# A decoder trunk with eight experts: transposes of the hidden activations in other PSUM banks, one gather at the end of an expert, and a down projection that ends with two pairs of blocks

## What is computed

```
x = x + sliding_window_attention(rms_norm(x, attn_norm), w_qkv, sinks, w_o)
x = x + swiglu(rms_norm(x, ffn_norm), w_gate, w_up, w_down)       # 2816 wide
x = x + pooling_mixer(rms_norm(x, pool_norm), pool_w, scale)      # trailing means, 4 groups
x = x + moe_swiglu(rms_norm(x, moe_norm), router, w_gate, w_up, w_down)
return rms_norm(x, final_norm)

def moe_swiglu(...):        # 8 experts, 3584 wide, the best 2 of each token
    logits = t @ w_router;  top 2;  gates = softmax(top 2)
    out = sum over e of combine[:, e] * ((silu(t @ w_gate[e]) * (t @ w_up[e])) @ w_down[e])
```

## Time and profile before

| | us |
|---|---|
| median of 3 runs | 1147.63 |
| the three runs | 1147.43, 1147.63, 1148.69 |
| the profiled execution | 1149.0 |
| its span in the trace | 1147.2 |
| PE matmul rows busy | 1127.3 (98%) |
| DVE, ACT busy | 313.4 (27%), 138.7 (12%) |
| DMA queue q1 | 83.3% of 16 engines' span |

### The profile page before, as it was taken

The page is one execution under the profiler, slowest core; times in us unless marked ns, Lnnn a source line. Parts: engine busy times, 40 slices in busy tenths (PEclk is TensorE's granted clock), DMA queues, the critical chain, the costliest instruction groups (busy, mean ns, idle before and its releaser), DMA issues.

```text
span 1147.2 us, 14885 instructions
## 1 busy us (share of the span) xinstructions
PE 1127.3 (98%) x6247; PEld 503.4 (44%) x6248; DVE 313.4 (27%) x561; ACT 138.7 (12%) x293; POOL 17.6 (2%) x59
## 2 busy tenths in 40 slices
PE   9999999999999999999999999999999999999997
PEld 8645566764653343353333335333333533333332
DVE  3556865666541110110201011021101101110102
ACT  1452011100131110000101000010100001110001
POOL 2300000000000000000000000000000000000000
PEclk9999999999999999999999999999999999999999
DMA  7535433447298999999999999999999999999995
GB/s 295 221 119 211 152 142 125 181 170 311 116 433 362 385 386 382 431 429 431 429 429 415 418 429 430 428 429 431 431 429 430 428 428 429 429 429 430 429 424 207
DMA packets 19414, 402.92 MB, mean 351 GB/s; under 512 B 3328, under 2 KB 3328, under 8 KB 4224
## 3 DMA queue, kind: packets, MB, share of 16 engines
q1 hardware_dynamic: 19328, 401.67, 83.3%
HBM read 400.61 MB, written 1.05 MB: 350 GB/s over the span
## 4 chain that ended last, share of the span: by engine, by line
PE 90%; DMA 7%; DVE 1%; ACT 1%; issue 0%; SPq 0%; DVEq 0%; ACTq 0%
PE bank L1686 32%; PE bank L1784 13%; PE bank L1447 12%; PE bank L1667 9%; PE bank L1482 6%; PE bank L1805 4%; DMA ring<-moe_w_up 4%; DMA ring<-moe_w_down 3%; PE bank L1394 2%; PE bank L1338 2%; PE bank L1646 1%; PE bank L1628 1%; DMA ring<-attn_w_qkv 1%; PE bank L1305 1%; PE bank L1748 1%; PE bank L1315 1%
## 5 line engine op out<-in xcount | busy, mean ns | idle before, releaser
L1686 PE MATMUL bank<-ring,arena 128*64 128x448 f32 x2048 | 391.3, 540 | 2.0 <-DMA ring<-moe_w_up 2.0
L1686 PEld LDWEIGHTS bank<-ring,arena 128*64 128x64 f32 x2048 | 144.7, 137 | 247.4 <-issue 244.3
L1784 PE MATMUL bank<-ring,arena 128*64 128x512 f32 x896 | 197.3, 595 | 2.5 <-DVE arena L1216 1.5
L1447 PE MATMUL bank<-ring 128*128 128x384 f32 (+1 forms) x448 | 134.4, 459 | 0.0
L1784 PEld LDWEIGHTS bank<-ring,arena 128*64 128x64 f32 x896 | 63.8, 137 | 124.3 <-issue 119.3
L1177 DVE TENSOR_TENSOR arena<-bank,arena 128x448 f32<-128x448 f32 x32 | 20.0, 625 | 332.9 <-PE bank L1686 332.9
L1447 PEld LDWEIGHTS bank<-ring 128*128 128x128 f32 x448 | 84.3, 190 | 45.8 <-issue 0.5
L1667 PE MATMUL bank<-ring,arena 128*32 128x448 f32 x1024 | 99.7, 541 | 0.0
L1227 DVE COPY arena<-bank 64x512 f32<-64x512 f32 x8 | 5.6, 694 | 228.4 <-PE bank L1784 228.4
L1667 PEld LDWEIGHTS bank<-ring,arena 128*32 128x32 f32 x1024 | 31.5, 110 | 66.6 <-issue 66.6
L867 DVE TENSOR_TENSOR ring<-ring 128x1536 f32<-128x1536 f32 (+2 forms) x35 | 53.2, 1540 | 10.3 <-PE bank L1381 9.3
(11 more groups left out here) (211 smaller groups left out, 675.3 us busy)
## 6 DMA issues: line engine op xcount, KB each, us to landing
ring<-moe_w_gate SPq DMA_DIRECT2D x32, 3584.0 KB, 24.3
ring<-moe_w_up SPq DMA_DIRECT2D x32, 3584.0 KB, 27.3
ring<-moe_w_down SPq DMA_DIRECT2D x29, 3584.0 KB, 27.5
ring<-ffn_w_gate SPq DMA_DIRECT2D x3, 3072.0 KB, 11.0
ring<-ffn_w_up SPq DMA_DIRECT2D x3, 3072.0 KB, 10.1
ring<-ffn_w_down SPq DMA_DIRECT2D x3, 3072.0 KB, 10.1
ring<-moe_w_down SPq DMA_DIRECT2D x3, 2048.0 KB, 31.4
ring<-moe_w_down SPq DMA_DIRECT2D x3, 1536.0 KB, 34.5
```

The source lines that it names most:

```text
L1447: last = mm(ffn_bank(m, i), b[lhs][:, k, :], b[rhs][:, k, :], start=k == 0, stop=k == 3)
L1686: last = mm(bank[2 * (j % 2) + up][64 * h:64 * h + 64, 0:FJ], xg[:, k, side:side + BASE], w[:, k, h, :], start=k == 0, stop=k == KD - 1)
L1784: last = mm(bank[2][64 * h:64 * h + 64, :], hg[:, i0 + i, half * BASE:half * BASE + BASE], w[:, i, h * BANK:h * BANK + BANK], start=d == 0 ...
```

## The change

- `STREAMED` is 9 in place of 8: pair 8 runs with the streamed ones, and the last round has two pairs per product, 9 and 10. Pair 9's sums lie in `ring[5]` in place of `nrm`; on DVE `scale_maps` moves behind `combine(9)`.
- The third down chunk is then free at `pair_done`, 9 in place of `prod_done`, 7, and SP loads the first expert's c = 3, which goes into that buffer, ahead of c = 1.
- `turn_banks`: at even places the batches of `hid` go to banks 0, 1, 6, 7 and those of `hidx` to banks 4 and 5; at odd places the banks stay as they were. So at even places batches b >= 2 don't wait for `hidx_ready`; the transposes of `hidx` do. In expert 0 they wait for the first gather's banks to have been read.
- Experts 1, 3, 5: the wait for `xg_ready` stands inside the branch that they don't take (they have no extra tokens). Batch b = 1 waits for the third part of `hid` in place of the fourth.
- Expert 0: the gather for expert 1 and the transposes of the combination weights stand behind the down products, with their copies on DVE (`keep_xg(1, 1)`) and ACT (`keep_combination`) moved likewise.

```
-STREAMED = 8
+STREAMED = 9
...
-HTR_BANK = (0, 1, 4, 5)
+def turn_banks(it):
+    return ((0, 1, 6, 7), (4, 5)) if isinstance(it, int) and it % 2 == 0 else ((0, 1, 4, 5), (6, 7))
...
-        read_by += [(pair_done, 3), (pair_done, 6), (prod_done, 7), (prod_done, 7), (mix_done, 2)]
+        read_by += [(pair_done, 3), (pair_done, 6), (pair_done, 9), (prod_done, 7), (mix_done, 2)]
...
-                for c in (2, 1, *range(3, PER_IT)) if first else range(PER_IT):
+                for c in (2, 3, 1, *range(4, PER_IT)) if first else range(PER_IT):
...
                 if looped:
                     gather(it + 1, 0)
-                elif it == 0:
-                    gather(1, 1)
...
-                    pe.wait_ge(hid_ready, 4 * it + min(b + 3, 4) if b < 2 else 4 * it + 4)
-                    if b >= 2:
+                    pe.wait_ge(hid_ready, 4 * it + (3 if b < 2 else 4))
+                    if b >= 2 and turned[b] < 6:
                         pe.wait_ge(hidx_ready, 4 * it + 4)
+                    elif b >= 2 and not looped and it == 0:
+                        pe.wait_ge(xg_ready, 2)
...
-                elif it < NE - 1:
-                    pe.wait_ge(xg_ready, 4 * ((it + 1) // 2) + 4)
                 with pe.If(ext > 0):
+                    if not looped:
+                        pe.wait_ge(hidx_ready, 4 * it + 4)
+                    if pair:
+                        pe.wait_ge(xg_ready, 4 * ((it + 1) // 2) + 4)
...
                     if d == 1:
                         pe.wait_ge(hgA_ready, 2 * it + 2)
                         pe.wait_ge(hgV_ready, 2 * it + 2)
-                        pe.wait_ge(dispw_ready, 2 * it + 2)
-                        for a in range(2):
...
+                        if looped or it > 0:
+                            combination(it)
...
+                if not looped and it == 0:
+                    combination(it)
+                    gather(1, 1)
                 return ext
```

More of the change, by code:

```diff
@@ L1715, in flag, with combination @@
                 return pe.value_load(one, min_val=0, max_val=1)
+            def combination(it):
+                pe.wait_ge(dispw_ready, 2 * it + 2)
+                if turn_banks(it)[1][0] == 4:
+                    pe.wait_ge(hgxA_ready, it + 1)
+                for a in range(2):
+                    for t in range(T):
+                        last = nc.tensor.transpose(bank[4][:, (2 * a + t) * P:(2 * a + t + 1) * P],
+                                                   dispw[:, t, a * P:a * P + P], ident[:, :])
+                last.then_inc(ctr_done, 1)
             def expert(it, extp, ext, looped=False):
```

33 lines of the change are left out of this document (18 added, 15 removed).

## The result

| | before, us | after, us |
|---|---|---|
| median of 14 runs each, on one chip | 1148.88 | 1150.37 |
| lowest to highest | 1147.43 to 1150.16 | 1148.32 to 1153.06 |
| the profiled execution | 1149.0 | 1150.26 |
| its span | 1147.2 | 1148.5 |

The ratio is 1.0015, with an interval of 1.0008 to 1.0022: by that ratio the changed kernel is 1.7 us slower (0.9 to 2.5), while the two medians differ by 1.5. The forecast was +0.9 us; the sign was right and the size about half of what was measured. The time itself lies just inside the stated range (1145.8 to 1150.4), but this says little: the forecast started from three runs with a median of 1147.63, and over 14 runs the kernel before has 1148.88.

A forecast was written before the change was run, and what follows sets the result against it. The prediction took the weight-chunk stream, last held up by PE at 647 us, as the bound; 1.5 + 0.5 - 0.33 - 0.77 = +0.9 us there gave 1148.5 us, range 1145.8 to 1150.4.

The forecast's parts named there:

- The bound: Whole kernel: a gapless stream of weight chunks to 1129 us sets the end, not PE.
- the anchor: End of expert 2, SP's issue of expert 3's c = 4 at 647.02 us: the stream's last standstill, forecast +0.9 us.
- Rival two: Stream does not hang on 647 us, gaps are transfer jitter, PE's changes vanish in the queue: 1147.6 us; chance 0.12.
- rival three: PE is the bound and the early chunk keeps its lead: -4.05 us, 1143.6 us; chance 0.07.
- The mixer: Mixer's first matmuls behind the last down-projection round: PE stops 1.44 us for the second norm, +1.5 us with the hand-over.
- Rival one: The mixer does not stall, the second norm is in time: anchor at -0.6, 1147.0 us; chance 0.14.
- The early chunk: First expert's c = 3, issued at 294.3 us, 12 us sooner: worth 0, as the queue runs dry at 358 us anyway.
- Expert 0: Gather and combination behind expert 0's down products: expert 1 starts 0.5 us later, bounds 0.3 to 1.0.
- Rival four: Expert 1 waits for its tokens behind DVE's copies: 2.8 us on top in full, 1151.3 us; chance 0.11.
- Odd experts: First down products of experts 1, 3, 5 wait less: -0.33 us each, only expert 1's ahead of the anchor.
- Even experts: Experts 2, 4, 6: batches 3 and 4 fill the `hidx_ready` wait, -0.77 us each, only expert 2's ahead of the anchor.
- The sum: Terms at the anchor, 1.5 + 0.5 - 0.33 - 0.77 = +0.9 us, carried by the stream to the end: 1148.5 us.

The follow-up runs named there:

- ffn_alone: Kernel before with only the down projection's part of the change (two pairs in the last round, early third expert chunk); 1150.96 us, ratio 1.0016.
- no_ffn: Changed kernel with the down projection's part undone (last round and third expert chunk as before), expert part kept; 1148.17 us, ratio 0.9995.
- no_ffn_warm: no_ffn with twelve identity transposes into an unused bank ahead of the last down step; 1148.78 us, ratio 0.9995.
- no_ffn_apart24: no_ffn with the extra down products of experts 2 and 4 also taken step by step, as expert 0's already were; 1146.07 us, ratio 0.9973.
- before_apart2: Kernel before with expert 2's extra down products taken step by step, as expert 0's already were; 1148.40 us, ratio 0.9991.
- gather_early: Changed kernel with expert 0's gather for expert 1 and combination transposes, and their copies, back in their old places; 1151.07 us, ratio 1.0010.
- after_again: The changed kernel itself, unaltered, run again on the chip of warm12_again; 1150.02 us, ratio 1.0010.
- late_chunk: Changed kernel with the first expert's c = 3 loaded as before, behind prod_done, 7 and behind c = 1; 1149.74 us, ratio 1.0008.
- cold: Kernel before with two of eight k-steps of expert 7's last up product left out, so PE waits longer for the last chunk; 1149.91 us, ratio 1.0007.
- no_ffn_apart2: no_ffn with expert 2's extra down products also taken step by step, as expert 0's already were; 1146.87 us, ratio 0.9979.
- warm12_again: Same code as warm12 (twelve filling transposes in the changed kernel), on the same chip as after_again; 1150.06 us, ratio 1.0010.
- no_ffn_apart2_ge: no_ffn_apart2 with expert 0's gather and combination transposes back in their old places; 1148.08 us, ratio 0.9989.
- warm12: Changed kernel with twelve identity transposes into an unused bank ahead of the last down step's wait; 1149.38 us, ratio 1.0005.
- no_ffn_apart: no_ffn with the extra down products of experts 2, 4 and 6 taken step by step, as expert 0's already were; 1147.28 us, ratio 0.9986.

## Why the prediction was right in part

- **The bound.** Right. The stream hangs on PE's time at 647 us: ffn_alone moves the anchor by 1.62 us and the last step by 1.46, no_ffn moves them by -1.16 and -1.64 (no_ffn_warm, though, has only the anchor's part), and with the gaps at the ends of experts 2 and 4 closed (no_ffn_apart24) PE no longer waits for a chunk. Rival two, a stream that does not hang on 647, falls. before_apart2 alone would not show it: its lead is lost again at expert 4, and its ratio, 0.9991, has an interval that reaches 1.0000. But with 2.1 us more work for PE it is not slower, and rival three, PE as the bound, falls by that. The Trainium skill ("Perfetto Trace Analysis", Identifying the Most-Contended Engine) puts the engine with the highest occupancy first, and calls matmul busy time a poor measure on TensorE. By its matmul rows PE is at 98%, yet the traces show that it did not set the time and became the bound only with the splits.
- **The mixer.** The idle time was 1.44 us, as worked out. Rival one falls. At the anchor the edit costs 1.62 to 1.69 us, forecast 1.5.
- **The early chunk.** 0, as said; issued at 294.00, forecast 294.3. The 1.2 us from an issue to its data, used on both sides of that sum, is about 1.0 in the traces.
- **Expert 0.** +0.32 us (gather_early), forecast 0.5. Rival four, a wait for expert 1's tokens, did not come: 445.72 + 3.71 us of gather, and the first product at 449.36.
- **Odd experts.** From the gather's first matmul to the down product, 501.75 to 508.94, it is 7.19 us and was 7.86 (499.90 to 507.76): -0.67, forecast -0.33, outside the bound of -0.5. The forecast had left 0.18 us of idle time ahead of the down product, as in expert 7; none is left in expert 1, and 0.58 us of the gain lies there. The other 0.09 stood ahead of the gather's second half. No run separates the moved wait from the looser wait of batch b = 1.
- **Even experts.** From the first transposes to the down product, expert 2 took 3.98 us (607.97 to 611.95) and takes 3.12 (609.14 to 612.26): 0.86 us less, forecast 0.77, just outside the bound of 0.85.
- **The sum.** +0.53 us at the anchor, forecast +0.9. Three of the four terms came out lower than forecast, the odd experts' most (by 0.34 us), so on that count the forecast was too high, not too low.
- **The failed step** is the last one: "The stream takes it to the end, 1129.36 + 0.9, and the last products and the norm behind it are unchanged." In the changed kernel's first trace both halves fail: the last chunk is there at 1129.27, 0.09 us sooner than before and not 0.9 later, and the last step takes 7.93 us, not 6.48. The gains of experts 3 to 6, put down as only making PE wait longer for chunks, made room for that: the waits for chunks sum to 5.38 us (1.06, 2.27, 2.05) where they were 2.75. I had looked for the growth near 942 us (3.33 of it with the wait at 935.51) and took the rest for free. Behind waits of 2 us the clock can fall, and in the last step nothing takes up the loss: +1.45 us in the profiled execution. In ffn_alone, without those gains, the step held to 0.2 us. What the step missed in the median is known only in part.
- **Where the rest of the loss is.** +0.53 at the anchor and +1.7 (0.9 to 2.5) in the median differ by 1.2 us. In the first trace it is the clock. In three others of the changed kernel or close to it (after_again, late_chunk, gather_early) the clock was full in the last step, and that step started later, at 1130.0 to 1131.6. The chunk that ended PE's wait near 944 us tells where. In after_again and gather_early it came 1.43 and 2.32 us later than in after (945.45 and 946.34 against 944.02), as the last chunk did: this time was lost ahead of 944 us, 0.53 and 0.61 of it before the mixer. In late_chunk it came 0.17 us sooner (943.85) and the last chunk 0.76 later, so there the loss lies behind 944 us, as in no_ffn_warm; what causes it no run shows. The gaps ahead of 660 us show a part of after_again's: the stretches below are 620 to 640 and 640 to 660 us of after, then of after_again. Their rates make a difference of 0.14 MB or some 0.3 us.

```profile
620.00:640.00 20.00, 20.00 (x124) 6.20 (x122) 0.00 (x0) 0.00 (x0) 0.00 (x0) 1.00 0.93 390
640.00:660.00 20.00, 20.00 (x130) 6.77 (x128) 2.81 (x5) 1.13 (x2) 0.00 (x0) 1.00 0.99 411
```

```profile
620.00:640.00 20.00, 20.00 (x122) 6.23 (x120) 0.00 (x0) 0.25 (x1) 0.00 (x0) 1.00 0.95 398
640.00:660.00 20.00, 20.00 (x130) 6.68 (x128) 2.81 (x5) 1.14 (x2) 0.00 (x0) 1.00 0.95 396
```

- **What stays open.** Whether the change makes such executions more frequent, or the few traces only happened to fall so, the runs don't settle; nor how often the fall comes last. On the second chip the changed kernel's ratio was 1.0010 (1.0001 to 1.0019), within reach of +0.53. The two halves' ratios, 1.0016 and 0.9995, add to about +1.3 us, between the two measurements of the whole. So part of the gap to +0.53 may be the noise of the timing. Settled are the slow-down, that the last round makes it (ffn_alone 1.0016, no_ffn 0.9995), and its path to the anchor.

## What to carry to other kernels

Where a stream of transfers sets the end, look for the last place where its queue runs dry, and work out each edit at that place; when it is closed, look for the next one, since it may lie just behind. PE's time gained behind that place is not neutral: it turns into longer waits, and a long wait can cost clock in the work that follows, which counts when that work is the last. Filling such a wait with work that nobody needs is free only where the wait is always longer than the filling. Making the bottleneck's buffers come free sooner, at the price of some slack on PE, brought 0.09% alone (at the edge of the noise) and up to 0.27% with the faster experts, 0.28% with the transposes besides; the faster experts alone brought 0.05%, which can't be told from nothing.

## What was not expected of the hardware

- The granted clock is not a matter of the wait's length alone, at these lengths: it fell to 0.50 after waits of 2.05 (after), 2.08 (cold, no_ffn_apart2) and 2.26 to 2.29 us (after_again, late_chunk, gather_early, warm12_again, no_ffn, no_ffn_warm, no_ffn_apart2_ge), and not after 1.96 (before, at 944.15), 2.27 (after, at 944.02), 2.26 (warm12, at 943.75) and 2.05 us (gather_early, at 1131.59, 6.42 us for the step). A fall costs 1.45 us in a down step and 1.57 to 1.70 in a gate or up product.
- Kernels that wait for the stream spread more between executions than those bound by PE: 4.7 us (1148.32 to 1153.06) in the changed one and 2.7 to 4.4 in the others on its line (before, after_again, late_chunk, no_ffn), against 0.9 in no_ffn_apart (1146.69 to 1147.62) and 1.7 in no_ffn_apart24 (1145.05 to 1146.79).
- Leaving work out made a kernel no faster and its profiled execution 1.4 us longer (cold).
